# Second block: wk and wv moved behind the neighbourhood attention, conv taps regrouped, one PSUM copy moved to ScalarE

## The reference, cut to what matters

```python
(a_glu, a_gate, nq, nk, nv, n_gate, wq, wk, wv, w_gate, merge) = split(h @ w_in[l])
# convolution branch: 31 taps along the sequence, one weight per channel
a = a_glu[..., :512] * sigmoid(a_glu[..., 512:])
a = depthwise_conv(a, conv_w, conv_b)                 # 31 taps
y_a = (silu(layer_norm_2(a)) * silu(a_gate)) @ w_proj_a
# neighbourhood attention: 8 rows x 16 columns of neighbours, and the 256 context keys
s = concat([q @ k_window * scale + bias, q @ k_ctx * scale]); p = softmax(s)
o_na = p_window @ v_window + p_ctx @ v_ctx
# window attention with wq, wk, wv: 8 query heads share 2 key/value heads, rope, a sink
y = sigmoid(g_a) * y_a + sigmoid(g_b) * y_b + sigmoid(g_c) * y_c
```

## Time and profile before

| | us |
|---|---|
| median of 3 runs | 3898.52 |
| lowest, highest | 3898.18, 3899.99 |
| the profiled execution | 3897.77 |
| its span in the trace | 3896.5 |

### The profile page before, as it was taken

One profiled execution on the slowest core, in us unless ns is written; L12 is line 12 of the kernel. 1 busy time (PEld: TensorE's weight loads), 2 busy tenths in 40 slices (PEclk: granted clock), 3 DMA queues, 4 the chain that ended last, 5 costly groups with the idle time before them and its releaser, 6 DMA issues.

```text
span 3896.5 us, 53469 instructions
## 1 busy us (share of the span) xinstructions
PE 3700.1 (95%) x21072; PEld 3099.0 (80%) x21072; DVE 2148.7 (55%) x3762; ACT 1478.9 (38%) x2556; POOL 1071.6 (28%) x744
## 2 busy tenths in 40 slices
PE   8999999999999999889999798899899999899999
PEld 7889878898889889559878687678788877678777
DVE  6555785675667777546333588721155328840442
ACT  3223554542234224445233413432244323353352
POOL 0003104341024003115101323933212323354223
PEclk9999999999999999999999899899999999899999
DMA  8565324455655565204333311012111212113112
GB/s 305 171 201 167 130 99 162 135 162 183 227 169 179 167 200 154 88 26 158 103 104 94 102 60 50 34 47 73 41 36 33 68 48 75 60 50 94 57 44 98
DMA packets 132154, 433.95 MB, mean 111 GB/s; under 512 B 14785, under 2 KB 14913, under 8 KB 131521
## 3 DMA queue, kind: packets, MB, share of 16 engines
q1 hardware_dynamic: 131904, 430.52, 34.3%
HBM read 428.36 MB, written 2.10 MB: 110 GB/s over the span
## 4 chain that ended last, share of the span: by engine, by line
PE 78%; DVE 10%; issue 5%; ACT 3%; POOL 3%; DMA 1%; SPq 0%; DVEq 0%; POOLq 0%; ACTq 0%
PE ps L645 21%; PE ps L647 21%; PE ps L646 21%; DVE cut L2333 4%; PE ps L2027 1%; POOL cut L1049 1%; POOL cut L569 1%; PE ps L1904 1%; PE ps L1988 1%; PE ps L2004 1%; PE ps L643 1%; PE ps L2010 1%; PE ps L1992 1%; PE ps L671 1%; PE ps L672 1%
## 5 line engine op out<-in xcount | busy, mean ns | idle before, releaser
L645 PE MATMUL ps<-cut 128*128 128x512 f32 (+1 forms) x5312 | 1875.5, 353 | 80.0 <-DVE cut L2196 18.6
L646 PE MATMUL ps<-cut 128*128 128x512 f32 (+1 forms) x5312 | 1852.9, 349 | 0.0
L647 PE MATMUL ps<-cut 128*128 128x512 f32 (+1 forms) x5312 | 1851.5, 349 | 0.0
L645 PEld LDWEIGHTS ps<-cut 128*128 128x128 f32 x5312 | 1019.5, 192 | 234.1 <-issue 71.6
L646 PEld LDWEIGHTS ps<-cut 128*128 128x128 f32 x5312 | 1020.7, 192 | 127.1 <-issue 4.2
L647 PEld LDWEIGHTS ps<-cut 128*128 128x128 f32 x5312 | 1019.0, 192 | 127.3
L569 POOL TENSOR_TENSOR cut<-cut 128x1024 fp32r<-128x1024 f32 (+3 forms) x269 | 591.5, 2202 | 1318.3 <-ACT cut L559 1317.6
L559 ACT ACTIVATE cut<-cut 128x1024 fp32r<-128x1024 f32 (+3 forms) x680 | 633.4, 939 | 835.8 <-PE ps L647 705.1
L569 DVE TENSOR_TENSOR cut<-cut 128x1024 fp32r<-128x1024 f32 (+3 forms) x411 | 499.1, 1216 | 436.7 <-ACT cut L559 436.5
L946 POOL TENSOR_TENSOR cut<-cut 128x512 fp32r<-128x512 f32 (+1 forms) x100 | 143.8, 1438 | 1089.0 <-ACT cut L905 1089.0
L2333 DVE SCALAR_TENSOR_TENSOR cut<-cut,cols 128x512 f32<-128x512 f32 (+1 forms) x330 | 280.3, 849 | 11.7
(11 more groups left out here) (327 smaller groups left out, 3454.9 us busy)
## 6 DMA issues: line engine op xcount, KB each, us to landing
cut<-in_ffn_in SPq DMA_DIRECT2D x200, 512.0 KB, 4.1
cut<-in_mod_w SPq DMA_DIRECT2D x136, 512.0 KB, 4.3
cut<-in_ffn_out SPq DMA_DIRECT2D x96, 384.0 KB, 3.2
cut<-in_ffn_out SPq DMA_DIRECT2D x96, 320.0 KB, 3.2
cut<-in_w_ada SPq DMA_DIRECT2D x48, 512.0 KB, 3.6
cut<-in_w_merge SPq DMA_DIRECT2D x48, 512.0 KB, 3.4
cut<-in_even_in SPq DMA_DIRECT2D x36, 512.0 KB, 3.6
cut<-in_proj SPq DMA_DIRECT2D x48, 256.0 KB, 2.6
```

The costliest lines, as they stand in the source:

```text
L645: te.matmul(o, hi[:, k - ka, w], xs[0], start=k == 0, stop=False)
L646: te.matmul(o, hi[:, k - ka, w], xs[1], start=False, stop=False)
L647: ins = te.matmul(o, lo[:, k - ka, w], xs[0], start=False, stop=last)
```

## The change

1. wk and wv leave their place behind wq. PE runs wk in step n of the neighbourhood jobs (n jobs, so behind the scores of all of them), wv in step n+1. The slab plan and SP's loads follow. The first two groups of agate, which stood in those steps, come after the jobs.
2. DVE does no taps between the neighbourhood jobs; what is left of them follows when its program has finished all jobs.
3. In layer 0 the first 256 positions of tile 3's second half go from POOL to DVE. POOL does 31 taps in place of 62, and splits the low part of agate's first slab after 12 of them.
4. In the neighbourhood jobs ACT and not DVE copies the transposed context exponentials. The window attention keeps DVE's copy.

```diff
@@ weight_plan
         lin(("nv", l), "w2_nv", (l,), range(4), low="g")
+        lin(("wk", l), "w2_wk", (l,), [0], low="g")
+        lin(("wv", l), "w2_wv", (l,), [0], low="g", toks=6)
...
-                lin(("wk", l), "w2_wk", (l,), [0], low="g")
-                lin(("wv", l), "w2_wv", (l,), [0], low="g", toks=6)
@@ pe_pairs
-                b = bank["p_tx", tag, i - 2] = yield from pe_take(("v_pt", tag, i - 2))
+                b = bank["p_tx", tag, i - 2] = yield from pe_take((copied_by[tag[0]], tag, i - 2))
...
-                te.wait_ge(*(yield "v_pt", tag, i - 3))
+                te.wait_ge(*(yield copied_by[tag[0]], tag, i - 3))
@@ act_pairs
+                if tag[0] == "na":
+                    se.wait_ge(*(yield "p_tx", tag, i - 2))
+                    se.activation(pbuf[:, :, w:w + 256], PS[bank["p_tx", tag, i - 2]][:, :].rearrange("p (a n) -> p a n", a=2),
+                                  ACT.Copy).then_inc(*sig("a_ptx", tag, i - 2))
@@ dve_pairs
-            if 0 <= i - 2 < n:
+            if 0 <= i - 2 < n and tag[0] == "wa":
@@ taps_of
-            which = [x[:3] for x in spans(l)] if t < 3 else [(527, 256, 512)] if l == 0 else [(256, 256, 256)]
+            which = [x[:3] for x in spans(l)] if t < 3 else [(256, 256, 256)] + [x[:3] for x in spans(l)[1:]]
@@ pe_second
-            0: lambda: nv(3), 1: lambda: values(2), 2: lambda: values(3), n: lambda: agate(0), n + 1: lambda: agate(1)}))
+            0: lambda: nv(3), 1: lambda: values(2), 2: lambda: values(3),
+            n: lambda: pe_linear(("wk", l), nrhs, GR, lambda m, gi: ("a_wk", l, gi), none),
+            n + 1: lambda: pe_linear_tok(("wv", l), nlhs, lambda t, c0: ("a_wv", l, t), none, 128)}))
+        yield from agate(0)
+        yield from agate(1)
         yield from pe_conv_means(l)
...
-        yield from pe_linear(("wk", l), nrhs, GR, lambda m, gi: ("a_wk", l, gi), none)
         yield from pe_head_sums(("wq", l), QG, 0)
-        yield from pe_linear_tok(("wv", l), nlhs, lambda t, c0: ("a_wv", l, t), none, 128)
@@ act_second
-            0: lambda: nv(3), 1: lambda: values(2), 2: lambda: values(3), 5: lambda: act_slabs(LIN["agate", l].ahead(0))}))
+            0: lambda: nv(3), 1: lambda: values(2), 2: lambda: values(3), 5: lambda: act_slabs(LIN["wk", l].ahead(0)),
+            n + 1: lambda: act_linear(("wk", l), to(WK, ("wk", l), "a_wk", GR))}))
+        yield from tok(("wv", l), WV, 128, 0, ("a_wv", l))
         yield from agate(0, 1)
@@ dve_second
-        yield from dve_pairs(("na", l), na_jobs(l), lambda i: dve_taps(l, 2))
+        yield from dve_pairs(("na", l), na_jobs(l), nothing)
         yield from dve_taps(l, 99)
@@ pool_second
-        yield from pool_taps(l)
-        yield from pool_linear(("agate", l), nothing)
+        yield from pool_taps(l, range(12))
+        yield from low_slabs("g", ge, LIN["wk", l].ahead(0))
+        yield from pool_taps(l, range(12, 31))
+        for name in (("wk", l), ("wv", l), ("agate", l)):
+            yield from pool_linear(name, nothing)
```

More of the change, by code:

```diff
@@ L2333, in dve_taps, with pool_taps @@
                     ve.scalar_tensor_tensor(out=o, in0=x, scalar=c, in1=o, op0=ALU.mult, op1=ALU.add).then_inc(*sig("v_tap", l, t, h0, j))
-    def pool_taps(l):
-        tmp, t, n = con("causal", 256, 256), 3, 512 if l == 0 else 256
+    def pool_taps(l, js):
+        tmp, t = con("causal", 256, 256), 3
         ge.wait_ge(*(yield "v_cp", l, 3, 0))
[L2338 to L2348, removed]
+        o = AG[:, t, 0:256]
+        for j in js:
+            i, w = CP[:, t, j:j + 256], col("conv2_w", 124 * l + 4 * j + t)
+            if j == 0:
+                ge.tensor_scalar(o, i, w, col("conv2_b", 4 * l + t), ALU.mult, ALU.add).then_inc(*sig("g_tap", l, 0))
+            else:
+                ge.tensor_scalar(tmp, i, w, None, ALU.mult).then_inc(*sig("g_tmp", l, j))
+                ge.wait_ge(*prev("g"))
+                ge.tensor_tensor(o, o, tmp, ALU.add).then_inc(*sig("g_tap", l, j))
+                ge.wait_ge(*prev("g"))
     def conv_made(l, t, h0):
@@ L2353, in conv_made @@
             return [("v_tap", l, t, h0, 30)]
-        return [("g_tap", l, 256, 30)] if l == 0 else [("g_tap", l, 0, 30), ("v_tap", l, 3, 256, 30)]
+        return [("g_tap", l, 30), ("v_tap", l, 3, 256, 30)]
     def conv_tmp(h0, i, n):
@@ L2524, in _build @@
     HEADS = (slice(0, 64), slice(64, 128))
+    copied_by = {"na": "a_ptx", "wa": "v_pt"}
     ROPES = {1: (0,), 2: (1, 2, 3)}
@@ L2734, in act_second @@
         yield from act_linear(("wq", l), to(WQ, ("wq", l), "a_wq", QG))
-        yield from act_linear(("wk", l), to(WK, ("wk", l), "a_wk", GR))
         se.wait_ge(*(yield "g_bl", "ngate", l, 3, len(QG) - 1))
@@ L2738, in act_second @@
         yield from act_head_sums(("wq", l), WQ, QG, 0)
-        yield from tok(("wv", l), WV, 128, 0, ("a_wv", l))
         def beside(m):
@@ L2825, in dve_second @@
         yield from dve_linear(("wq", l), nothing)
-        yield from dve_linear(("wk", l), nothing)
         yield from dve_head_sums(("wq", l), QG, 0)
-        yield from low_slabs("v", ve, LIN["wv", l].ahead(0))
         def beside(m):
@@ L2874, in pool_second @@
         yield from pool_branch(l, "ngate", QG)
-        for name in (("wq", l), ("wk", l), ("wv", l)):
-            yield from pool_linear(name, nothing)
+        yield from pool_linear(("wq", l), nothing)
         yield from pool_merge(l, 1, MERGES1)
@@ L2897, in sp_second @@
                 yield from sp_linear(("nv", l), (3,))
-        yield from sp_linear(("agate", l))
+        for name in (("wk", l), ("wv", l), ("agate", l)):
+            yield from sp_linear(name)
         for kind, m in MERGES:
             yield from sp_linear((kind, l, 0, m))
-        for name in (("ngate", l), ("wq", l), ("wk", l), ("wv", l)):
+        for name in (("ngate", l), ("wq", l)):
             yield from sp_linear(name)
```

## The result

| | before | after |
|---|---|---|
| median, us | 3898.87 (4 runs) | 3930.39 (4 runs) |
| lowest, highest | 3898.18, 3899.99 | 3928.00, 3933.07 |
| the profiled execution | 3897.77 | 3933.07 |
| its span in the trace | 3896.5 | 3931.8 |

The ratio is 1.0079, with a 95% interval of 1.0067 to 1.0091. The change makes the kernel 31.5 us slower. The forecast was 3896.2, and its range ended at 3907: it was wrong.

What follows compares the result with a forecast made beforehand. Taps between jobs were taken to hold PE up, PE being the bound without them. Shorter jobs and moved wk and wv, against the tap stall, clock and bank waits, gave -2.3 us: 3896.2, range 3888 to 3907.

Steps and rivals of the forecast that it cites:

- Jobs of layer 0 (-36.3): Layer 0's neighbourhood jobs: without taps PE sets the pace; steps of 13.0 and 52.2 us, -36.3, bounds -33 to -38.
- B: Jobs: ScalarE's new copy sets the step; at 0.3 us a step +10, near 3906; chance 8%.
- D: Layer 0's jobs: transposes keep all 24 steps at clock 0.50; +70, over 3960; chance 1%.
- Jobs of layer 1 (-5.3): Layer 1's jobs: one step held up by eight taps falls to its own work, -5.3 us, bounds -4 and -6.
- wk and wv, 24.7 moved: Behind wq in each layer: moving wk (8.53) and wv (16.13) wins back 24.7 us there, low end 22.5.
- Bank waits (3.2 and 3.1): New PE waits at banks ahead of wv and agate: 3.2 and 3.1 us, bounds 2 and 5 a layer.
- The taps behind the jobs: Layer 0: 93 taps start behind wv, take 54.2 us, delay the third agate group by 21.1; layer 1 nothing.
- The clock (+3.5): After PE's stall at layer 0's conv means: work at the lower clock costs 3.5 us, bounds 1.5 to 5.7.
- Rival C: After PE's stalls: clock at 0.50 for 30 us of work, loss 15, near 3908; 8% with waits around wq.
- The sum: All terms together: layer 0 -0.1, layer 1 -2.2, together -2.3 us, median 3896.2.

Runs made afterwards that it cites:

- e1: The changed kernel, but ACT copies wk right behind its step n, ahead of the result of job n-3: 3893.75 us, ratio 0.9988.
- e9: The kernel of e3, but wk and wv and their slabs back behind wq: 3887.20 us, ratio 0.9972.
- e3: The changed kernel, but PE does wk and wv after all jobs and their value products: 3867.29 us, ratio 0.9924.
- e8: The kernel of e3, with a wait added on PE ahead of wk, for the third tap behind the jobs: 3873.92 us, ratio 0.9929.
- e2: The kernel before the change, with a wait added on PE ahead of wv, for the reciprocal of the head sums: 3942.89 us, ratio 1.0109.
- e4: The changed kernel, but DVE again copies the context exponentials in the neighbourhood jobs (part 4 undone): 3912.71 us, ratio 1.0034.
- e10: The kernel of e3 measured once more, unchanged, on another occasion: 3870.75 us, ratio 0.9926.
- e7: The kernel of e3, but in layer 0 GpSimd does the first 12 taps of tile 3's second span: 3865.26 us, ratio 0.9905.

## Why the prediction was wrong, step by step

**Jobs of layer 0 (-36.3).** From the third job's scores (2419.73, 2424.21 after) to the last transpose (2521.48, 2493.93) 101.75 us passed before, and 69.72 after: -32.0, a little outside the bounds. (The terms of the forecast, 13.0 and 52.2, end at 2484.9 and not at 2485.2; that makes 0.3.) PE is idle for 3.3 us in all. It waits 1.54 us for ACT's copies of the value product, where I had put 0.3, and 0.85 once for DVE; the rest are pauses of some tenths. The mechanism was right: with the taps gone PE is the bound and its clock is at 1.00. Rivals B and D fall: PE was busy 63.65 of 65.40 us.

**Jobs of layer 1 (-5.3).** From the first to the last scores 62.0 us passed before and 58.0 after: -4.0, at the edge of the bounds (-4 to -6).

**wk and wv, 24.7 moved.** The winning back behind wq was right, if at the low end: from the third agate group to the window attention after is 23.3 and 22.1 us shorter than before, and e1 22.8 and 23.7. The price at the new place was not. I took wv at 16.13 us from a row where nothing stands ahead of it, and in the next paragraph put a wait of 1.7 ahead of it. This is **the step that failed**: wv cost 28.6 and 30.5 there, 12.5 and 14.4 us more. In layer 0 DVE's taps wait for it besides.

**Bank waits (3.2 and 3.1).** 1.65 + 1.49 and 1.81 + 1.49: right as lengths. But a wait's price is not its length. e1 takes only the first of each away and is 15.1 us shorter in layer 0 and 20.0 in layer 1. In layer 1, 1.8 of the 20.0 are the wait, 14.2 wv itself, 2.2 the last products behind it, still at the lower clock; the last 1.7 or so come from a later pause of 4.9 us that both kernels have, after which the clock was low 3.4 us longer in this profile of after.

**The taps behind the jobs.** The order was read rightly: the taps start behind wv and the last products, take 54.0 us, and PE stands in two pieces. They begin at 2538.3 in place of 2515.5. Of these 22.8 us, 4.7 are the later start of the whole execution, 4.3 the jobs, and 12.5 wv's clock.

**The clock (+3.5).** I let the clock fall only where PE stands long, and took the bounds from two restarts, 11.4 and 3.1 us. After the two stalls of 16.0 and 11.5 us it was low for 17.1 and 13.7 us in all, most of it idle. PE worked in 4.0 and 5.2 us of that, and half of it, some 4.6, is what the two restarts cost: so this term was right within its bounds. Rival C had the right resource and the wrong place. (By its own sum it would have left the forecast's band from 27 us at the lower clock on, not from 24.)

**The sum.** e1 is the change with the one wait removed: +0.8 in layer 0 and -4.2 in layer 1, where the forecast had -0.1 and -2.2. The forecast had that wait in its sum, though (1.65 and 1.81), and 2.5 us of e1's layer 1 lie ahead of the jobs; with both put right e1 is 2 to 3 us above the forecast in each layer. So all other terms together were off by some 5 us, and some 30 of the 34 us of the miss are this one interaction. The range could have held it: the trace of before has no row of wv behind a wait, so its cost there was unknown, between once and twice 16.1 us. I took the lower end as certain. A rival with wv at the lower level in both layers, +16 each, would have stood at 3928.

What stays open is why the clock does not come back within wv. The runs show when it did not, not why.

In steps, layer 0 and layer 1: taps out of the jobs, copies on ACT -5.8 and -4.3 (e9); wk and wv behind the jobs -20.5 and about -1 (e3); wk and wv moved into the jobs' last two steps, so that the taps wait for them, +27.0 and +1.8 (e1); the wait ahead of wv +15.1 and +20.0 (after).

## What to carry to other kernels

A short wait directly ahead of a long run of narrow matmuls may be priced by that run, not by its own length (here 12 to 15 us more for waits of 1.3 to 4.3): look at what PE does behind each new wait, and put other work there (here wk, in e8), or free the bank earlier (e1). Work that is meant to cover another engine must not stand, on PE, ahead of what that engine's queue is waiting for. And when a change cancels itself out on paper, as here 42 us of jobs against a stall, try each part alone: the same parts in another order gave 30 to 35 us.

## What the runs showed that I had not expected

- The 144 matmuls of 128x128 of wv run at 1.00 where no wait or one of 0.75 us stands directly ahead of them. In five cases, with waits of 1.32 to 4.34 us, the clock fell in the wait or within 3 us of wv's start and did not come back before wv's end: 28.6 to 31.0 us, at a mean of 0.50 to 0.54. It came back 3.8 us into agate (layer 0 of after), 4.2 and 4.8 us into the 128x512 matmuls of the merge (e2), and within wk (e8), but also in the 64-row value products behind wv, 4.2 us after its end (layer 1 of after). So it did not take wide matmuls every time. The Trainium skill describes in "TensorE: Matmul & The Clock Gate", section "A second HAM failure mode: psum-queue depth-cycling", how frequent short idle times between groups of matmuls, at the PSUM banks, let the clock swing between its levels. Here it is otherwise in part: one wait of 1.65 us at a bank was enough, and the clock does not swing, but stays low for the rest of wv.
- A copy of 0.6 us on ScalarE moved the whole time by 18 us (e4). In the one profile, the wait ahead of wv grew by it from 0.75 to 1.65 us in layer 0, and wv's clock fell only after the longer one.
- A VectorE instruction on 128x2 elements, 0.17 us elsewhere, took 1.80 us while GpSimd subtracted a slab. The first row is GpSimd's, the second VectorE's; both end at 2426.1.

```profile
2423.70 2.36 POOL L569 TENSOR_TENSOR cut<-cut 128x1024 fp32r<-128x1024 f32 x1 [19.56 <-ACT cut L559]
```

```profile
2424.29 1.80 DVE L2090 TENSOR_SCALAR st<-st 128x2 f32<-128x2 f32 x1
```

  The Trainium skill says in "SBUF — State Buffer", section "Who interferes with whom", that a tensor_scalar too can take the port pair that VectorE shares with GpSimd, and that the one that comes second is blocked until the other is done; this row agrees.
- The stretch ahead of the change differs by 7 us between two profiles of the same kernel (e3 and e10), and by up to 11 between profiles of kernels with the same instructions there. A difference of 2 us was visible within a layer (e7 against e3) and not in the medians.
